# First stage of a fused decoder block: all of x loaded by four wide transfers, narrow products started later, first weights' low parts on GpSimd

## What is computed

```python
u = rmsnorm(h, norm_mix[i])          # x * rsqrt(mean(x*x) + 1e-6) * gain
z = u @ w_in[i]                      # 2048 x 6464
...
h = h + jnp.concatenate([y_rw, y_fox], axis=-1) @ w_out[i]
u = rmsnorm(h, norm_mlp[i])
h = h + jnp.square(jax.nn.relu(u @ w_ff1[i])) @ w_ff2[i]
```

## Time and profile before

| | |
|---|---|
| median of 3 runs | 2726.4 us (2724.23 to 2728.66) |
| the profiled execution | 2730.28 us |
| span of its trace, first to last instruction | 2728.7 us |
| TensorE busy | 2635.3 us, 97% of the span |
| VectorE, ScalarE, GpSimd busy | 1245.8, 893.6, 192.1 us |
| first large matmul (L577) starts at | 43.33 us |

### The profile page before, as it was taken

The page is one execution under the profiler, slowest core; times in us unless marked ns, Lnnn a source line. Parts: engine busy times, 40 slices in busy tenths (PEclk is TensorE's granted clock), DMA queues, the critical chain, the costliest instruction groups (busy, mean ns, idle before and its releaser), DMA issues.

```text
span 2728.7 us, 46014 instructions
## 1 busy us (share of the span) xinstructions
PE 2635.3 (97%) x17796; PEld 2130.5 (78%) x17796; DVE 1245.8 (46%) x1646; ACT 893.6 (33%) x1330; POOL 192.1 (7%) x220
## 2 busy tenths in 40 slices
PE   7999999999588999999999999999999999999997
PEld 5777777777477678888888888888888888888885
DVE  5565666666444555443223442233422344334444
ACT  4443444444455324222122222122212222233333
POOL 0000000000233002000000000000000000111010
PEclk9999999999899999999999999999999999999998
DMA  7555454555522333333333333333333333333333
GB/s 199 149 154 159 142 143 143 158 156 164 176 95 94 105 101 92 101 92 100 92 100 93 99 93 99 93 99 95 97 96 96 98 94 100 92 100 103 100 96 87
DMA packets 530289, 310.04 MB, mean 114 GB/s; under 512 B 56399, under 2 KB 508737, under 8 KB 529217
## 3 DMA queue, kind: packets, MB, share of 16 engines
q1 hardware_dynamic: 480785, 264.95, 34.0%
q0 software_dynamic: 9264, 31.04, 3.3%
q10 hardware_dynamic: 40192, 13.40, 1.8%
HBM read 273.04 MB, written 36.31 MB: 113 GB/s over the span
## 4 chain that ended last, share of the span: by engine, by line
issue 59%; PE 28%; DVE 4%; DMA 3%; ACT 3%; POOL 2%; SPq 0%; POOLq 0%; DVEq 0%; ACTq 0%
PE acc L577 5%; PE acc L579 4%; PE acc L578 4%; PE acc L984 2%; PE acc L986 2%; PE acc L985 2%; POOL sumsq L2093 2%; ACT w_hi L1116 1%; DMA z_d<-ev 1%; PE bank L765 1%; PE bank L677 1%; PE acc L775 1%; PE bank L775 1%; DVE pr L1677 1%; PE bank L794 1%
## 5 line engine op out<-in xcount | busy, mean ns | idle before, releaser
L1548 DVE TENSOR_TENSOR w_lo<-w_raw,w_hi 128x1024 fp32r<-128x1024 f32 x420 | 521.3, 1241 | 1109.4 <-ACT w_hi L1116 1107.3
L1116 ACT ACTIVATE w_hi<-w_raw 128x1024 fp32r<-128x1024 f32 x420 | 444.7, 1059 | 1169.3 <-PE acc L579 1120.7
L577 PE MATMUL acc<-a_hi,w_hi 128*128 128x512 f32 x1824 | 720.0, 395 | 2.1 <-DVE w_lo L1548 2.0
L579 PE MATMUL acc<-a_hi,w_lo 128*128 128x512 f32 x1824 | 711.0, 390 | 0.0
L578 PE MATMUL acc<-a_lo,w_hi 128*128 128x512 f32 x1824 | 710.8, 390 | 0.0
L577 PE MATMUL acc<-b_hi,w_hi 128*128 128x512 f32 x1280 | 498.5, 389 | 0.0
L579 PE MATMUL acc<-b_hi,w_lo 128*128 128x512 f32 x1280 | 498.0, 389 | 0.0
L578 PE MATMUL acc<-b_lo,w_hi 128*128 128x512 f32 x1280 | 498.0, 389 | 0.0
L577 PEld LDWEIGHTS acc<-a_hi,w_hi 128*128 128x128 f32 x1824 | 342.8, 188 | 98.2 <-issue 22.4
L579 PEld LDWEIGHTS acc<-a_hi,w_lo 128*128 128x128 f32 x1824 | 342.7, 188 | 72.3
L578 PEld LDWEIGHTS acc<-a_lo,w_hi 128*128 128x128 f32 x1824 | 343.0, 188 | 71.2 <-issue 1.9
(11 more groups left out here) (284 smaller groups left out, 2048.6 us busy)
## 6 DMA issues: line engine op xcount, KB each, us to landing
w_raw<-in_w_ff SPq DMA_DIRECT2D x256, 512.0 KB, 3.9
w_raw<-in_w_in SPq DMA_DIRECT2D x100, 512.0 KB, 3.9
w_raw<-in_w_out SPq DMA_DIRECT2D x32, 512.0 KB, 3.9
w_raw<-in_w_ple_gate SPq DMA_DIRECT2D x32, 512.0 KB, 3.9
z_d<-ev POOLq DMA_DIRECT2D x50, 256.0 KB, 3.5
x_c<-ab_d SPq DMA_DIRECT2D x8, 1024.0 KB, 4.8
ab_d<-ab ACTq DMA_DIRECT2D x7, 1024.0 KB, 7.1
x_t<-ab_d SPq DMA_DIRECT2D x9, 512.0 KB, 3.7
```

What stands on the lines that cost most here:

```text
L577: mm(dst, wh, hi[:, kt, :], start=kt == 0, stop=False)
L579: last = mm(dst, wl, hi[:, kt, :], start=False, stop=kt == KT - 1)
L1116: A(w_hi[:, s, :, :], w_raw[:, s, :, :], ACT.Copy).then_inc(sg("w_hi_ready"), 1)
L1548: V.tensor_tensor(w_lo[:, s, :, 0:width], w_raw[:, s, :, 0:width], w_hi[:, s, :, 0:width].bitcast(F32), ALU.subtract).then_inc(sg("w_split ...
```

## The change

- All of x gets a buffer of its own (`xin` of 128 by 4 by 2048) and is loaded by four transfers of 2, 4, 5 and 5 tiles, without waits. One wait of PE per transfer takes the place of one per tile.
- The first transfer of constants is cut to the identity and the ones (256 columns); the rest of the constants follows x.
- SP loads the first two weight units right behind x, and then all 16 rows of parameters.
- The two transfers of the narrow weights are issued by ACT as its first instructions. ACT splits them behind tile 5 instead of 2.
- Narrow products start behind the transposes of tile 8: two tiles' worth behind each of tiles 8 to 11, one behind each of 12 to 15, four at the end as before.
- The parameters are transposed behind the last narrow product instead of ahead of the last four.
- ACT copies the first unit behind tile 11 (was 9) and the second behind tile 13 (was behind the last).
- GpSimd, not DVE, makes the low parts of the narrow weights and of the first two units. Its four stores of `h` come behind these in its program. DVE waits for both units before it goes on to the mean square.

```diff
+    x_blocks = (0, 2, 6, 11, KT)
-    xin = sb("xin", [P, 4, T // P, P], at)
+    xin = sb("xin", [P, T // P, D], at)
@@ sync
-            sp.dma_start(cst[:, :], consts[:, 0:C_RESET]).then_inc(sg("first_landed"), 16)
+            sp.dma_start(cst[:, 0:C_MASK], consts[:, 0:C_MASK]).then_inc(sg("first_landed"), 16)
+            for b, (f0, f1) in enumerate(zip(x_blocks, x_blocks[1:])):
+                sp.dma_start(xin[:, :, f0 * P:f1 * P], x_v[:, :, f0 * P:f1 * P]).then_inc(sg(f"x_landed{b}"), 16)
+            sp.dma_start(cst[:, C_MASK:], consts[:, C_MASK:C_RESET]).then_inc(sg("parameters_landed"), 16)
-            for f in range(KT):
-                if f >= 4:
-                    sp.wait_ge(sg("x_transposed"), f + 1)
-                sp.dma_start(xin[:, f % 4, :, :], x_v[:, :, f * P:(f + 1) * P]).then_inc(sg(f"x_landed{f % 4}"), 16)
...
+            for s in range(2):
+                first_unit(s)
+            for dst, src in others:
+                sp.dma_start(dst, src).then_inc(sg("parameters_landed"), 16)
@@ tensor
-                b = f % 4
-                pe.wait_ge(sg(f"x_landed{b}"), 16 * (f // 4) + 16)
+                if f in x_blocks:
+                    pe.wait_ge(sg(f"x_landed{x_blocks.index(f)}"), 16)
                 pe.wait_ge(sg("xt_taken"), f + 1)
-                if f > 3:
-                    narrow(f - 4)
+                if f >= 8:
+                    for k in range(2 * (f - 8) if f < 12 else f - 4, min(2 * (f - 7), f - 3)):
+                        narrow(k)
...
             narrow(KT - 1).then_inc(sg("narrow_done"), 1)
+            pe.wait_ge(sg("gain_ready"), 1)
+            pe.wait_ge(sg("parameters_landed"), 16 * N_PAR)
+            for k in range(2):
+                last = nc.tensor.transpose(bank[4][:, k * P:(k + 1) * P], prow[:, k, :], ident)
@@ scalar
+            for cols, n0, n in ((slice(0, 32), N_SHIFT - 32, 32), (slice(32, 48), N_SHIFT + 3 * DR, 16)):
+                act.dma_start(nw[:, :, cols], w_in_v[:, :, n0:n0 + n]).then_inc(sg("narrow_landed"), 16)
-                if f == 2:
+                if f == 5:
                     act.wait_ge(sg("narrow_landed"), 32)
-                if f == 9:
+                if f == 11:
                     hi_unit(0, 0, 0)
-            hi_unit(1, 0, 0)
+                if f == 13:
+                    hi_unit(1, 0, 0)
@@ vector
-                if f == 3:
-                    dve.wait_ge(sg("narrow_hi_ready"), 1)
-                    V.tensor_tensor(nw_lo[:, :, :], nw[:, :, :], nw_hi[:, :, :].bitcast(F32), ALU.subtract).then_inc(sg("narrow_split"), 1)
-                if f == 11:
-                    lo_unit(0, Z_ODD)
-            lo_unit(1, Z_ODD + 1)
+            dve.wait_ge(sg("w_split"), Z_ODD + 4)
@@ gpsimd, ahead of the stores of h
+            pool.wait_ge(sg("narrow_hi_ready"), 1)
+            G.tensor_tensor(nw_lo[:, :, :], nw[:, :, :], nw_hi[:, :, :].bitcast(F32), ALU.subtract).then_inc(sg("narrow_split"), 1)
+            for s in range(2):
+                pool.wait_ge(sg("w_hi_ready"), Z_ODD + s + 1)
+                G.tensor_tensor(w_lo[:, s, :, :], w_raw[:, s, :, :], w_hi[:, s, :, :].bitcast(F32), ALU.subtract).then_inc(sg("w_split"), 1)
```

More of the change, by code:

```diff
@@ L618, in _ @@
             for f in range(KT):
-                b = f % 4
-                pe.wait_ge(sg(f"x_landed{b}"), 16 * (f // 4) + 16)
+                if f in x_blocks:
+                    pe.wait_ge(sg(f"x_landed{x_blocks.index(f)}"), 16)
                 pe.wait_ge(sg("xt_taken"), f + 1)
                 for q in range(T // P):
-                    last = nc.tensor.transpose(bank[1 + f % 2][:, q * P:(q + 1) * P], xin[:, b, q, :], ident)
+                    last = nc.tensor.transpose(bank[1 + f % 2][:, q * P:(q + 1) * P], xin[:, q, f * P:(f + 1) * P], ident)
                 last.then_inc(sg("x_transposed"), 1)
@@ L639, in _ @@
             narrow(KT - 1).then_inc(sg("narrow_done"), 1)
+            pe.wait_ge(sg("gain_ready"), 1)
+            pe.wait_ge(sg("parameters_landed"), 16 * N_PAR)
+            for k in range(2):
+                last = nc.tensor.transpose(bank[4][:, k * P:(k + 1) * P], prow[:, k, :], ident)
+            last.then_inc(sg("parameters_transposed"), 1)
             pe.wait_ge(sg("x_sums_taken"), 1)
```

## The result

The changed kernel takes 2735.14 us in the median of 6 runs (2732.84 to 2740.87), beside 2727.02 in the median of 5 runs of the kernel before: a ratio of 1.0029, 95% interval 1.0018 to 1.0041. The profiled execution took 2735.29 us with a span of 2733.7, against 2730.28 and 2728.7 before: 5.0 us more. The first large matmul starts at 48.49 us instead of 43.33, 5.16 later. So the whole difference between the two traces arose ahead of it, and what comes behind passed it on about one to one, as the prediction supposed. `after` is the changed kernel.

A forecast was written before the change was run, and what follows sets the result against it. TensorE, busy 97%, bounds the kernel, so only time before the first large matmul counts. Stage floor -8.1, PE's order +3.05, port +3.5, start +0.2, parameters +0.2: 1.1 us earlier, 2725.3 us; range 2721.6 to 2728.9.

The forecast's parts named there:

- the dearest of which: Rival: both narrow issues on ACT take 3.92 us, first copy at 10.4, +3.05, 2728.4 us; chance 0.08.
- first copy: Start of the x stage: DVE's first copy at 7.35 instead of 7.15, +0.2 us, bounds 6.5 and 10.4.
- narrow weights there by 17.5: x stage: ACT splits the narrow weights behind square 5, 10.2 us after the first copy; no cost for their landing.
- narrow products 0 and 1: PE, behind tile 8's transposes: first two narrow products at the fast clock, 0.69 us each, done 13.8 after first copy.
- the rest of PE's order, up to copy 10: Tiles 8 to 12: PE's doubled narrow products outpace DVE's 1.50 us a tile; copy 12 loses 3.05 us in all.
- two units at the port: Tiles 12 and 13: DVE operations with two SBUF inputs stop while GpSimd works; 1.75 us per unit, +3.5.
- last copy to first large matmul: End of the x stage: chain of 5.6 us unchanged, plus 0.2 us for two parameter transposes.
- The start and the narrow weights: Stage start: narrow issues leave ACT ready at about 7.3; 0.21 MB less ahead of x; first copy 7.35, +0.2 us.
- The clock falls: Rival: TensorE at 1.2 GHz when the first narrow product starts, +2.1 us, 2727.4 us; chance 0.27.
- The hole of before: First 60 us of the kernel before: one wide gap where DVE's copies stand while x lands and PE is slow.
- What was hidden: Costs put at nothing: x's loads behind tile 6, ACT's unit copies, the units' readiness, the late stores of h.
- Behind 43 us: Span after the first large matmul taken as unchanged, passing shifts one to one; rival that it eats the gain: 0.05.

The follow-up runs named there:

- narrow_by_sp: Changed kernel, but SP issues the two narrow transfers behind x's second transfer, not ACT; 2730.66 us, 1.0006 of before.
- both: Changed kernel with SP issuing the narrow transfers behind x's second and VectorE making the first two units' low parts; 2726.28 us, 0.9997 of before.
- units_on_dve: Changed kernel, but VectorE again makes the low parts of the first two weight units; 2731.07 us, 1.0007 of before.
- filler: Changed kernel with sixteen narrow matmuls into an unused bank ahead of the last sum of squares; 2734.50 us, one run.
- units_gpsimd_alone: Kernel before with only the first two units' low parts moved to GpSimd, high parts behind tiles 11 and 13; 2731.86 us, 1.0017 of before.
- wide_x_alone: Kernel before with x resident in four transfers, narrow transfers on SP behind the second, units and parameters behind x; 2728.87 us, 1.0003 of before.
- order_alone: Kernel before with only the narrow products moved: from tile 8 on, two behind each of tiles 8 to 11; 2729.05 us, 1.0002 of before.
- both_warm: Changed kernel with SP's narrow transfers, VectorE's unit low parts and filler matmuls between early transposes; 2733.43 us, 1.0020 of before.

## Why the prediction was wrong

It had 6.3 us too little at the first large matmul (42.2 against 48.49), and the median of 2735.14 lies above every rival, the dearest of which was 2728.4. Two of its steps failed. It put the landing of the narrow weights at nothing: they landed at 20.4 us instead of by 17.5 and held up x's first transfer. And it took TensorE's clock as kept at the fast level, but it was at 1.2 GHz up to the first two narrow products and again at the end. By its own steps, against the trace:

| step of the forecast | forecast | after | too late by |
|---|---|---|---|
| first copy | 7.35 | 8.26 | 0.9 |
| x's second transfer in time | no wait | lands 10.54, copy 2 at 11.70 | 0.44 |
| sum of squares ahead of tile 6 | hidden | at the slow level | 0.53 |
| narrow weights there by 17.5 | not costed | 20.4, copy 8 at 23.59 | 1.24 |
| narrow products 0 and 1 | 0.69 each | 1.18 and 1.28, and tile 9's transposes at the slow level | 1.65 |
| the rest of PE's order, up to copy 10 | as computed | | 0.2 |
| two units at the port | 3.5 | 1.31 + 1.97 = 3.28 | -0.2 |
| last copy to first large matmul | 5.8 | 7.34 | 1.54 |

**The start and the narrow weights: failed.** The prediction took the price of the two narrow transfers from how long their issue took on SP and asked when ACT would be free. ACT was free at 5.66, sooner than the 7.3 that it took, but that was the wrong question. It never asked when they land, beside 4 MB of x in wide rows on the other queue. The second landed 18.0 us after issue, and the two delayed x's first transfer by 1.6. The bytes that it summed (0.21 MB less ahead of x) said nothing about rows of 64 and 128 bytes. narrow_by_sp and both show the price: 5.6 and 3.5 us, of which the late start, the wait and the clock are parts.

**The clock: failed as a forecast, right as a rival.** "The clock falls" had 0.27 and +2.1 us. Its condition came true, the level at product 0 was 1.2 GHz, but by another way: the clock had not fallen there, it had not risen since the first transposes. This cost 0.53 + 1.65 in the sum of squares and the first two products. Behind PE's idle time at the end it did fall, for another 1.54: 3.7 us in all. Against it the prediction set that 1.8 us of idling around 38 left the clock alone. That holds: 1.8 us before, and in units_on_dve, costs nothing, while 3.9 does in all five kernels in which it stands. What it missed is that its own port term makes the idle time at the end longer: the last copy moves and PE has run out of transposes by 39.24. The second fall follows from a number that was already in the sum.

The prediction set a rule of the Trainium skill aside here, "TensorE: Matmul & The Clock Gate", Part 4, that transposes don't count as busy for the clock. In after and both the transposes stayed at 1.0 to 1.12 for four from the first to the last ahead of the narrow products, as the rule would have it. In before (0.66 at 13.5) and in narrow_by_sp (0.66 at 11.73) four were fast behind sixteen and twenty transposes, and in units_on_dve twelve from 17.24 took 2.65, so that the level rose among them. In filler, which up to there is the same program as after, four took 0.66 at 13.94 behind twenty; the level was then lost again in the 4.08 us that PE stood for the low parts, and product 0 ran at 1.2 GHz all the same. So transposes can bring the fast level with nothing else ahead of them but 0.6 us of small matmuls for the gain, against the rule as the prediction gave it, and the same code does not always do so. What decides stays open.

**The port: right.** Folds 12 and 13 ended 0.55 us behind GpSimd's subtractions and were 1.31 and 1.97 us late, 3.28 against 3.5; fold 6 likewise beside the narrow split (1.80). units_gpsimd_alone shows it apart from all else. The same subtraction took 2.37 to 2.67 us, inside the bounds of 2.1 to 3.0.

**What bounds the kernel: half right.** The hole of before was read as x that lands late and a slow clock. wide_x_alone and order_alone show two limits, x's four buffers and PE's standing in order at the first narrow product. The prediction's sum was safe from this, since the change removes both.

**What was hidden: right.** No copy waited for x behind tile 6. The stores of `h` went out at 40.61 to 43.76 and nobody waited for them; the store of `zo_d` was issued at 54.92. The units were ready long before the first large product.

**Behind 43 us: nearly right.** In the traces the 5.16 us became 5.0 of span. The medians differ by 8.1, with an interval of 4.9 to 11.2, so 5.2 lies inside it. In the experiments, too, the median's distance from before lies between 0.7 us below and 3.7 above the stage's, mostly above (units_on_dve: +3.6 beside +1.4; narrow_by_sp: +3.2 beside -0.5), both_warm aside. That is within each one's interval. One reason is the yardstick: the profiled execution of before, at 2730.28, is itself 3.3 us above the median of its runs, that of after 0.15. Where in its trace these 3.3 us lie is not known. So the distances from before in the table are less sure than those from after.

## What to carry to other kernels

Ask of a moved transfer when it lands among what runs beside it on the other queues, not only how long its issue takes: here short rows next to wide ones on another queue landed after 18.0 us instead of 7.2, and they made the wide ones 1.6 us later. When a term of the sum lets an engine idle for longer, carry that into the clock of what it does next; 3.9 us of idling cost TensorE 1.5 us here, 1.8 us cost none. Before you move work from VectorE to GpSimd, see whether what VectorE does meanwhile reads two operands from SBUF: here such folds of 0.75 us took 2.06 and 2.72. And where one trace of each kernel is compared, look for two traces of the same code first: here they differ by 2 us within one stage.

## What the runs showed that was not expected

- Of two transfers of 0.39 MB in all, of 128-byte and 64-byte rows, the later landed 7.2 us after issue when queued on SP behind part of x (5.2 to 9.2 in the other kernels with SP), 18.0 to 20.5 on ACT's queue beside wide rows of x, and 10.3 there beside 512-byte rows. The Trainium skill, "DMA: Bandwidth & Descriptors", section "Queues, rings and completion order", says that a DMA engine takes turns between queues packet by packet; the direction of these three numbers agrees with it, if a turn of short rows carries less. No trace here shows the turns themselves, nor why the first of the two transfers landed after 6.3 us in after and only the second was late.
- The same two issues on ACT took 2.52 us at the start and 9.97 us behind the gain's copy, and ACT computed nothing meanwhile.
- The granted clock reads 1.00 in the stretches ahead of its first recorded change, while four transposes take 1.05 to 1.12 us instead of 0.60 (after, 14 to 20 us). At the start of a span the level is to be read from durations.
- Matmuls of 48 columns on data already there kept the clock through 3.9 us in which PE had nothing else to do, and did not delay the sum behind them: PE still stood 0.19 us for ACT's square.
